# The sums of squares of three norms in one product each, and a first norm half a piece later

## The reference, cut to what matters

```
def rmsnorm(x, g):
    return x * rsqrt(mean(x * x, axis=-1) + EPS) * g

h = rmsnorm(x, norm_g)                       # first norm, 1024 channels
(qa, ka, va, ga, qb, kb, vb, ab, gb, cq, ckv, kr, gc, mg) = split_cols(h @ w_in)
...
log_a = log_sigmoid(ab @ w_alpha + b_alpha) / 16     # decay of the linear attention
q_c = rmsnorm(cq, cq_g) @ w_uq               # first latent norm, 256 channels
kv  = rmsnorm(ckv, ckv_g) @ w_ukv            # second latent norm, 128 channels
```

## Time and profile before

| | before |
|---|---|
| median of three runs | 922.04 us |
| profiled execution | 921.61 us, span 919.8 us, granted TensorE clock 0.999 |
| PE busy | 912.6 us (99%), 5074 matmuls |
| DVE busy | 613.2 us (67%) |
| ACT busy | 390.7 us (42%) |
| POOL busy | 32.3 us (4%) |
| DMA | 111.02 MB, mean 121 GB/s |

### The profile page before, as it was taken

How to read it: one execution, slowest core, us unless ns; L and a number is a source line. 1 busy time by engine, 2 the same in 40 slices (tenths; PEclk the granted TensorE clock), 3 DMA queues, 4 the chain that set the end, 5 groups by cost and what they waited for, 6 DMA issues and landing times.

```text
span 919.8 us, 13078 instructions
## 1 busy us (share of the span) xinstructions
PE 912.6 (99%) x5074; PEld 750.7 (82%) x5074; DVE 613.2 (67%) x1017; ACT 390.7 (42%) x726; POOL 32.3 (4%) x69
## 2 busy tenths in 40 slices
PE   9999999999999999999999999999999999999997
PEld 7988888888888777888889888888888887778886
DVE  6986468338656877575458855664567668876835
ACT  6563344225543455432444523442363435463324
POOL 0000000000000001000000000000000000100000
PEclk9999999999999999999999999999999999999999
DMA  8334325332534345422233433253235233444542
GB/s 316 101 106 130 115 70 160 95 110 80 152 115 133 93 132 161 138 91 92 92 115 95 124 93 115 69 161 103 80 115 162 102 115 116 130 148 137 151 124 91
DMA packets 46989, 111.02 MB, mean 121 GB/s; under 512 B 12656, under 2 KB 15760, under 8 KB 46800
## 3 DMA queue, kind: packets, MB, share of 16 engines
q1 hardware_dynamic: 40928, 100.72, 34.6%
q10 hardware_dynamic: 3920, 5.25, 2.1%
q0 software_dynamic: 2080, 4.22, 1.6%
HBM read 85.43 MB, written 2.24 MB: 95 GB/s over the span
## 4 chain that ended last, share of the span: by engine, by line
PE 99%; DMA 0%; ACT 0%; issue 0%; DVE 0%; POOLq 0%
PE ring L689 76%; PE nat L689 9%; PE nat L898 3%; PE aux L921 2%; PE nat L877 1%; PE nat L704 1%; PE nat L703 1%; PE nat L706 1%; PE ring L704 1%; PE ring L703 1%; PE ring L706 1%; PE nat L782 1%; DMA par_all<-params 0%; PE ring L759 0%; PE ring L769 0%; PE nat L849 0%
## 5 line engine op out<-in xcount | busy, mean ns | idle before, releaser
L689 PE MATMUL ring<-act_hi,w_hi 128*128 128x512 f32 x784 | 307.5, 392 | 0.0
L689 PE MATMUL ring<-act_lo,w_hi 128*128 128x512 f32 x784 | 305.4, 390 | 0.0
L689 PE MATMUL ring<-act_hi,w_lo 128*128 128x512 f32 x784 | 305.2, 389 | 0.0
L938 ACT ACTIVATE w_hi<-raw 128x1024 fp32r<-128x1024 f32 x152 | 161.5, 1064 | 330.2 <-PE ring L689 257.4
L1279 DVE TENSOR_TENSOR w_lo<-raw,w_hi 128x1024 fp32r<-128x1024 f32 x152 | 184.6, 1216 | 98.2 <-ACT w_hi L938 98.0
L689 PEld LDWEIGHTS ring<-act_hi,w_hi 128*128 128x128 f32 x784 | 147.1, 188 | 37.3 <-issue 7.3
L689 PEld LDWEIGHTS ring<-act_hi,w_lo 128*128 128x128 f32 x784 | 147.1, 188 | 31.1
L689 PEld LDWEIGHTS ring<-act_lo,w_hi 128*128 128x128 f32 x784 | 147.2, 188 | 29.7
L1665 DVE SCALAR_TENSOR_TENSOR gates<-ring,rstd 128x512 f32<-128x512 f32 x72 | 49.4, 686 | 79.2 <-PE ring L689 79.0
L689 PE MATMUL ring<-y_hi,w_hi 128*128 128x512 f32 x192 | 74.9, 390 | 0.0
L689 PE MATMUL ring<-y_hi,w_lo 128*128 128x512 f32 x192 | 74.7, 389 | 0.0
(11 more groups left out here) (240 smaller groups left out, 1040.4 us busy)
## 6 DMA issues: line engine op xcount, KB each, us to landing
raw<-pieces SPq DMA_DIRECT2D x152, 512.0 KB, 3.5
bank_g<-work SPq DMA_DIRECT2D x80, 64.0 KB, 2.6
lat<-work SPq DMA_DIRECT2D x48, 64.0 KB, 2.7
bank_g<-work POOLq DMA_DIRECT2D x40, 64.0 KB, 2.4
bank_g<-work ACTq DMA_DIRECT2D x40, 64.0 KB, 3.2
xt<-x_t SPq DMA_DIRECT2D x8, 256.0 KB, 5.3
bank_a<-work SPq DMA_DIRECT2D x32, 64.0 KB, 2.0
bank_g<-bank_a SPq DMA_DIRECT2D x16, 128.0 KB, 3.9
```

What stands on the lines that cost most here:

```text
L689: mm = pe.matmul(dst, stationary, moving, start=start and i == 0, stop=stop and i == 2)
L938: nc.scalar.activation(w_hi[:, n % HL, :], raw[:, n % RAW, :], ACT.Copy).then_inc(hi_split.sem, 1)
```

## The change

Each set of partial sums is folded before the split: ACT copies the upper 64 partitions down, and DVE adds them to the lower 64. The folded sums are split on 64 partitions; the high part stands in the lower and the low part in the upper half of one 128-row tile, so one product with the ones takes both. That makes new steps "sum_fold" (ahead of "sum_split") and "latent_sums" (behind "log_lo"). For the latents the copies down take the place of the two copies to `lat_hi` on ACT and the additions that of the two subtractions in "gla_gate" on DVE; ACT's new copies to `lat_hi` stand behind that of log_hi.

In the list, "rms" moves from the middle of PN1[0] behind its end, "early" from ahead of PN1[1] into its middle, "latent" 1 and what follows it half a piece later. The parameters are loaded from ACT's queue behind the first weights instead of from POOL's, and WARM is 6 instead of 5.

```diff
-WARM = 5
+WARM = 6
@@ make_schedule
     piece(PX)
+    step(("sum_fold", 0))
     half(PC[0], 0)
     step(("sum_split", 0))
     half(PC[0], 1)
     piece(PC[1])
-    half(PN1[0], 0)
+    piece(PN1[0])
     step(("rms", 0))
-    half(PN1[0], 1)
+    half(PN1[1], 0)
     step(("early", 0))
-    piece(PN1[1])
+    half(PN1[1], 1)
     step(("rstd_nat", 0), ("lat_sum", 0))
...
-    step(("log_lo", 0))
+    step(("log_lo", 0), ("latent_sums", 0))
...
-    step(("latent", 1))
     half(PN2[0], 0)
-    step(("latent_lo", 0))
+    step(("latent", 1), ("latent_lo", 0))
     half(PN2[0], 1)
+    half(PN2[1], 0)
     step(("latent_norm", 1), ("latent_hi", 1))
-    piece(PN2[1])
+    half(PN2[1], 1)
     step(("latent_lo", 1))
@@ TensorE, "rms" ("latent" likewise)
-                        pe.matmul(aux[:, :], ones_r[:, :], lat_hi[:, 1, :], start=True, stop=False)
-                        mm = pe.matmul(aux[:, :], ones_r[:, :], lat_lo[:, 1, :], start=False, stop=True)
+                        mm = pe.matmul(aux[:, :], ones_r[:, :], lat_hi[:, 1, :], start=True, stop=True)
@@ ScalarE
                 act.dma_start(raw[:, p, cols], pieces[p, :, cols]).then_inc(head_loaded[n].sem, 16)
+                if n == 0:
+                    act.dma_start(par_all[:, :, :], params).then_inc(par_loaded.sem, 16)
...
                         if p == PC[2]:
...
-                            nc.scalar.activation(lat_hi[:, 0, :], sq_sum, ACT.Copy).then_inc(lat_sq_hi.sem, 1)
+                            act.wait_ge(sum_folded.sem, sum_folded.at(layer, 1))
+                            nc.scalar.activation(lat_upper[0], sq_sum[high, :], ACT.Copy).then_inc(lat_moved.sem, 1)
                             nc.scalar.activation(sq[0], latent[:, 2, :], ACT.Square).then_inc(lat_sq.sem, 1)
                             act.wait_ge(lat_sq.sem, lat_sq.at(layer, 3))
-                            nc.scalar.activation(lat_hi[:, 2, :], sq[0], ACT.Copy).then_inc(lat_sq_hi.sem, 1)
+                            nc.scalar.activation(lat_upper[1], sq[0][high, :], ACT.Copy).then_inc(lat_moved.sem, 1)
...
                     elif name == "sum_split":
+                        act.wait_ge(sum_folded.sem, sum_folded.at(layer, 1))
+                        nc.scalar.activation(lat_hi[low, 1, :], sq_sum[low, :], ACT.Copy).then_inc(sum_hi.sem, 1)
+                    elif name == "sum_fold":
                         act.wait_ge(x_acc.sem, x_acc.at(layer, LATE))
-                        nc.scalar.activation(lat_hi[:, 1, :], sq_sum, ACT.Copy).then_inc(sum_hi.sem, 1)
+                        if layer > 0:
+                            act.wait_ge(merge_lo.sem, merge_lo.at(layer - 1, KT))
+                        else:
+                            act.wait_ge(proj_done.sem, proj_done.at(0, 0))
+                        nc.scalar.activation(sum_upper, sq_sum[high, :], ACT.Copy).then_inc(sum_moved.sem, 1)
@@ ScalarE, "gla_gate"
                         nc.scalar.activation(log_hi, log_a, ACT.Copy).then_inc(log_hi_set.sem, 1)
+                        for n, summed in enumerate((sq_sum, sq[0])):
+                            act.wait_ge(lat_folded.sem, lat_folded.at(layer, n + 1))
+                            nc.scalar.activation(lat_hi[low, 2 * n, :], summed[low, :], ACT.Copy).then_inc(lat_sq_hi.sem, 1)
@@ GpSimd
-            pool.dma_start(par_all[:, :, :], params).then_inc(par_loaded.sem, 16)
@@ VectorE, "sum_split"
-                        nc.vector.tensor_tensor(lat_lo[:, 1, :], sq_sum, lat_hi[:, 1, :].bitcast(F32),
+                        nc.vector.tensor_tensor(lat_hi[high, 1, :], sq_sum[low, :], lat_hi[low, 1, :].bitcast(F32),
                                                 ALU.subtract).then_inc(sum_lo.sem, 1)
+                    elif name == "sum_fold":
+                        dve.wait_ge(sum_moved.sem, sum_moved.at(layer, 1))
+                        nc.vector.tensor_tensor(sq_sum[low, :], sq_sum[low, :], sum_upper, ALU.add).then_inc(sum_folded.sem, 1)
@@ VectorE, "gla_gate"
-                        for n, squares in enumerate((sq_sum, sq[0])):
-                            dve.wait_ge(lat_sq_hi.sem, lat_sq_hi.at(layer, n + 1))
-                            nc.vector.tensor_tensor(lat_lo[:, 2 * n, :], squares, lat_hi[:, 2 * n, :].bitcast(F32),
-                                                    ALU.subtract).then_inc(lat_sq_lo.sem, 1)
+                        for n, summed in enumerate((sq_sum, sq[0])):
+                            dve.wait_ge(lat_moved.sem, lat_moved.at(layer, n + 1))
+                            nc.vector.tensor_tensor(summed[low, :], summed[low, :], lat_upper[n], ALU.add).then_inc(lat_folded.sem, 1)
...
+                    elif name == "latent_sums":
+                        for n, summed in enumerate((sq_sum, sq[0])):
+                            dve.wait_ge(lat_sq_hi.sem, lat_sq_hi.at(layer, n + 1))
+                            nc.vector.tensor_tensor(lat_hi[high, 2 * n, :], summed[low, :], lat_hi[low, 2 * n, :].bitcast(F32),
+                                                    ALU.subtract).then_inc(lat_sq_lo.sem, 1)
```

More of the change, by code:

```diff
@@ L377, in build_hybrid_trunk @@
         lat_rstd = merged[:, 6, :]
+        low, high = slice(0, 64), slice(64, 128)
+        sum_upper, lat_upper = merged[low, 7, :], (merged[low, 7, :], merged[low, 1, :])
         state = merged[:, 0:4, :].rearrange("p a (c j v) -> p (a c) j v", c=2, j=2)
@@ L443, in build_hybrid_trunk @@
         warm_set = sig("warm_set", 0)
+        sum_moved, sum_folded = sig("sum_moved", 1), sig("sum_folded", 1)
+        lat_moved, lat_folded = sig("lat_moved", 2), sig("lat_folded", 2)
         sum_hi, sum_lo = sig("sum_hi", 1), sig("sum_lo", 1)
@@ L837, in _ @@
                         pe.wait_ge(lat_sq_lo.sem, lat_sq_lo.at(layer, i + 1))
-                        pe.matmul(aux[:, :], ones_r[:, :], lat_hi[:, 2 * i, :], start=True, stop=False)
-                        mm = pe.matmul(aux[:, :], ones_r[:, :], lat_lo[:, 2 * i, :], start=False, stop=True)
+                        mm = pe.matmul(aux[:, :], ones_r[:, :], lat_hi[:, 2 * i, :], start=True, stop=True)
                     elif name == "gla_state":
```

## The result

The changed kernel takes 926.91 us (median of six, 925.84 to 927.15) against 921.84 us for the kernel before (six, 921.65 to 923.25): ratio 1.0051, 95% interval 1.0038 to 1.0064, so slower by 5.1 us. The forecast was 926.1 us. The profiled execution has a span of 925.3 us against 919.8, 5.5 more.

The account below looks back on a forecast made before the run. PE (TensorE) was taken as the bound, holding 99% of the chain of waits. 3.0 + 1.7 + 0.74 - 0.92 - 0.4 = +4.1 us gave 925.7 us profiled, 926.1 us on the median; range 925.0 to 927.3 us.

Parts of the forecast that it names:

- start: Program start: parameters land at 4.8 us, two more warming passes, first product at 6.1 to 6.5 us; -0.4 us.
- first norm, layer 0: Ahead of PC[2]: refining 3.2 us later shifts DVE's full block, so PE waits for piece 7's low part; +3.0 us.
- clock, layer 0: Rival: PE's 3.1 us idle ahead of PC[2] drops its clock to 1.2 GHz; 2.2 us more, 928.3 us; 10%.
- gla_decay, layer 0: PE waits in gla_decay for log_lo, late from DVE's shift and ACT's two more latent copies; +0.36 us.
- first norm, layer 1: Ahead of PC[2]: refining 4.3 us later, 2.7 us to spare, PE waits for piece 7's low part; +1.7 us.
- gla_decay, layer 1: PE waits in gla_decay for log_lo, ending at 517.72 us when PE comes at 517.44; +0.38 us.
- latents' products: The latents' sums lose four products with the ones on PE, 0.23 us each; -0.92 us.
- Folding hidden: Layer 0: folded sum ready at about 26.2 us, PE asks at 27.9; all hidden, 1.7 us to spare.

Follow-up runs that it names:

- the swap on ACT: The changed kernel with ACT's high part of piece 6 moved behind the first norm's table load, logarithm and exponential: 921.71 us, ratio to before 0.9992.
- the filled wait: The changed kernel with twelve unused products on PE in layer 0 ahead of PC[2], where PE otherwise idles: 925.71 us, ratio to before 1.0035.
- the shorter wait: The changed kernel without the first norm's table load in layer 0: 924.50 us, ratio to before 1.0022.
- the part measured alone: The kernel before with only the parameters moved to ACT's queue, five warming matmuls kept: 921.25 us, ratio to before 0.9993.

## Why the prediction came out as it did

The time lies 0.8 us above the forecast and within its range. Some luck is in that: the forecast's own range, 925.0 to 927.3 us, was drawn without the clock, which cost 1.7 us, and 0.36 us of that was made up by a wait in gla_decay that did not come. Differences of start times between the two profiles, layer by layer:

| term | predicted | measured | from |
|---|---|---|---|
| start | -0.4 | -0.17 | third product 7.18 to 7.01 |
| first norm, layer 0 | +3.0 | +2.88 | PC[2] 42.56 to 45.27, less the start |
| clock, layer 0 | rival, 10% | +1.71 | first product of gla_decay 62.15 to 66.57, less what PC[2] has |
| gla_decay, layer 0 | +0.36 | 0 | no wait |
| first norm, layer 1 | +1.7 | +1.52 | PC[2] 496.17 to 501.65, less 3.96 carried in |
| gla_decay, layer 1 | +0.38 | +0.45 | 515.75 to 521.68, less 5.48 |
| latents' products | -0.92 | -0.92 | 4 x 0.23, in 3.96 = 4.42 - 0.46 and in the end |
| sum | +4.1 | +5.5 | span 919.8 to 925.3 |

**Folding hidden: right.** The sum was ready by 26.1 us (25.38 + 0.69) and PE took it at 27.75.

**The first norm: right in place, mechanism and size.** The order on ACT, 3 and 6 us of idle DVE, and 3.0 and 1.6 us of waiting PE are in the profile, and the swap on ACT showed that the split ahead of the table load decides.

**The clock: the step that failed.** "PE idles about 3.1 us ahead of PC[2]" was right, but the fall was given a chance of 10%, because PE had gone on at full pace behind a gap of 0.8 us. The row says 0.66 us, and it was no evidence for a gap more than four times as long. The rival was in fact what happened, beside the forecast: at 1.6 to 1.7 us it was a little cheaper than the 2.2 it was priced at, because the lower level lasted 3.4 us (46.8 to 50.2), not 4.4. The Trainium skill, "TensorE: Matmul & The Clock Gate", section "What's actually happening", has an idle TensorE go back to the lower clock. The trace agrees for this wait of 3.03 us, and the filled wait shows the converse: the granted clock stayed at 1.00 where PE was kept busy.

**gla_decay: right in layer 1, wrong in layer 0,** where PE, slowed by the clock, came at 66.57 us and log_lo had ended at 64.60 + 1.22 = 65.82. With the clock up, as in the filled wait and the shorter wait, PE does wait there for log_lo, 0.3 and 0.36 us by starts. In layer 1 the wait is 0.36 of the 0.45 us in the table; the other 0.1 is the longer first step of PC[2] behind its own wait (0.34 us instead of 0.23).

**The start: the size.** The parameters took 4.2 us from issue to landing, about as long as from POOL's queue (4.3), and ACT used them from 5.44 us in this execution, where the forecast let them land at 4.8. So less of the gain came here; over many executions the part measured alone gives about 0.5.

## What to carry to other kernels

When a step is moved in an order that several engines walk, list for each engine the instructions that it is moved past; here one 1.06 us copy that waits for the matrix engine, with a 1.28 us table load behind it, cost 5 us: with the copy behind the norm the same kernel is as fast as the one before. A full engine passes a delay on whole, so look for the first consumer with little slack behind it rather than at the step itself. And price a long wait of the matrix engine twice, once for its length and once for the clock behind it.

## What the runs showed of the hardware

The granted clock fell only after PE had been at work again for 1.3 us (from 45.27 us to the step behind 46.54, where the slow steps begin), and stayed at 0.5 for 3.4 us though PE was busy all that time. Waits of 1.20, 1.60 and 1.61 us were followed by a granted clock of 1.00, one of 3.03 us was not.

An ACT copy of 512 elements per partition took 0.63 us on 64 partitions, down to other partitions or in place, and 0.63 us on 128; the DVE subtraction on 64 took 0.69 us. Folding to half the partitions made no single instruction cheaper: all that it saved were matmuls.
